# Five expert loads cut into sixteen-row and eight-row transfers, and a rearranged start of the value projection, in a one-core encoder layer

## The reference

```python
xn = rms_norm(h, norm1_w)
proj = xn @ w_in
q, k, v, r, a_low, hy_in, gates = jnp.split(proj, IN_SPLITS, axis=-1)
o_gla = gla_branch(q, k, v, r, a_low, gla_gate_w2, gla_gate_b, gla_norm_w)
kern = hyena_filters(L, hy_freq, hy_ffn_w1, ...)      # sin(fr * (z @ w1 + b1)), then w2, then w3
merged = sigmoid(g_gla) * (o_gla @ w_branch_gla) + sigmoid(g_hy) * (o_hy @ w_branch_hy)
h = h + merged @ w_out
for e in range(N_EXPERTS):                            # 32 experts
    gu = ht @ w_gate_up[e] + b_gate_up[e]             # 1024 x 2048 weights
    act = gate * sigmoid(SWIGLU_ALPHA * gate) * (up + 1.0)
    out = out + combine[:, e:e + 1] * (act @ w_down[e] + b_down[e])
```

## Time and profile before

| | |
|---|---|
| median of three runs | 1238.31 us |
| profiled execution, its own time | 1237.29 us |
| its span, first to last instruction | 1235.4 us |
| granted TensorE clock, mean | 0.999 |
| TensorE matmul busy | 1160.8 us (94%) |
| DVE, ACT busy | 420.2 us (34%), 266.9 us (22%) |
| bytes moved by DMA | 455.25 MB, mean 368 GB/s |

### The profile page before, as it was taken

The page is one execution under the profiler, slowest core; times in us unless marked ns, Lnnn a source line. Parts: engine busy times, 40 slices in busy tenths (PEclk is TensorE's granted clock), DMA queues, the critical chain, the costliest instruction groups (busy, mean ns, idle before and its releaser), DMA issues.

```text
span 1235.4 us, 13704 instructions
## 1 busy us (share of the span) xinstructions
PE 1160.8 (94%) x5828; PEld 599.6 (49%) x5828; DVE 420.2 (34%) x703; ACT 266.9 (22%) x422; POOL 0.2 (0%) x4
## 2 busy tenths in 40 slices
PE   7999999999999999999999889888988898889987
PEld 6899968888533443443343324333433333333332
DVE  6777878756421221222112112111221121111112
ACT  6866546344210000010010001000100010000002
POOL 0000000000000000000000000000000000000000
PEclk9999999999999999999999999999999999999999
DMA  9454425698999999999999999999999999999996
GB/s 322 147 157 151 148 91 171 217 399 340 365 425 428 427 428 428 427 429 425 429 426 429 428 428 428 427 428 428 427 428 425 429 427 429 427 429 427 427 426 263
DMA packets 67292, 455.25 MB, mean 368 GB/s; under 512 B 6970, under 2 KB 23771, under 8 KB 39966
## 3 DMA queue, kind: packets, MB, share of 16 engines
q1 hardware_dynamic: 65654, 454.06, 89.8%
q10 hardware_dynamic: 1576, 0.29, 0.1%
HBM read 453.29 MB, written 1.05 MB: 368 GB/s over the span
## 4 chain that ended last, share of the span: by engine, by line
PE 64%; DMA 32%; DVE 2%; issue 1%; ACT 1%; DVEq 0%; ACTq 0%
DMA ring<-in_w_gate_up 28%; PE bank L1201 18%; PE bank L1219 12%; PE total L902 6%; PE bank L902 5%; PE total L890 4%; PE bank L890 4%; DMA ring<-in_w_down 3%; PE bank L960 2%; PE bank L1187 2%; PE bank L979 1%; PE total L1233 1%; PE total L1201 1%; PE bank L1208 1%; PE total L950 1%
## 5 line engine op out<-in xcount | busy, mean ns | idle before, releaser
L1201 PE MATMUL bank<-ring,hy_area 128*64 128x512 f32 x1984 | 444.6, 595 | 43.2 <-DMA ring<-in_w_gate_up 43.2
L1201 PEld LDWEIGHTS bank<-ring,hy_area 128*64 128x64 f32 x1984 | 136.8, 137 | 331.4 <-issue 244.6
L1219 PE MATMUL bank<-ring,xn_area 128*64 128x512 f32 x992 | 220.1, 595 | 0.3 <-DMA ring<-in_w_down 0.3
L2119 DVE TENSOR_SCALAR qk_area<-bank 128x512 f32<-128x512 f32 x31 | 21.4, 692 | 361.3 <-PE bank L1201 361.3
L1219 PEld LDWEIGHTS bank<-ring,xn_area 128*64 128x64 f32 x992 | 68.4, 137 | 134.6 <-issue 122.8
L1682 ACT ACTIVATE qk_area<-qk_area 128x512 f32<-128x512 f32 x32 | 20.2, 630 | 456.7 <-DVE qk_area L2119 456.7
L2130 DVE SCALAR_TENSOR_TENSOR xn_area_r<-bank,tmp_area,xn_area_r 128x512 fp32r<-128x512 f32 x31 | 23.3, 751 | 200.5 <-ACT xn_area_r L1693 200.5
L1823 DVE TENSOR_TENSOR front_r<-ring,slot_r 128x1024 fp32r<-128x1024 f32 x60 | 73.1, 1222 | 22.2 <-ACT slot_r L1493 22.2
L1493 ACT CAST slot_r<-ring 128x1024 fp32r<-128x1024 f32 x60 | 62.8, 1049 | 43.5 <-PE bank L902 23.2
L1693 ACT ACTIVATE xn_area_r<-bank,tmp_area 128x512 fp32r<-128x512 f32 x31 | 21.3, 687 | 234.9 <-PE bank L1219 221.0
L979 PE MATMUL bank<-tmp_area_r 128*128 128x512 f32 x124 | 38.0, 426 | 12.8 <-issue 8.6
(11 more groups left out here) (397 smaller groups left out, 1253.2 us busy)
## 6 DMA issues: line engine op xcount, KB each, us to landing
ring<-in_w_gate_up SPq DMA_DIRECT2D x116, 2048.0 KB, 37.0
ring<-in_w_down SPq DMA_DIRECT2D x54, 2048.0 KB, 38.9
ring<-in_w_in SPq DMA_DIRECT2D x31, 1024.0 KB, 5.7
ring<-in_w_gate_up SPq DMA_DIRECT2D x22, 1024.0 KB, 9.4
ring<-in_w_down SPq DMA_DIRECT2D x19, 1024.0 KB, 9.9
ring<-in_w_branch_gla SPq DMA_DIRECT2D x4, 1024.0 KB, 5.2
ring<-in_w_branch_hy SPq DMA_DIRECT2D x4, 1024.0 KB, 7.7
ring<-in_w_out SPq DMA_DIRECT2D x4, 1024.0 KB, 6.3
```

Of the source, the lines that this page charges most:

```text
L1201: last = pe.matmul(to[bk][half * CAP:(half + 1) * CAP, :], xeT[:, j, q, :], where(j, c), start=False, stop=(j == GU_CH - 1), skip_group_ch ...
L1219: last = pe.matmul(banks[to][half * CAP:(half + 1) * CAP, :], half_of(turned, f), where(j, c * D + half * 512), start=(f == 0), stop=(f == ...
L2119: nc.vector.tensor_scalar(gate, made[0][:, :], LIMIT, None, ALU.min).then_inc(gate_ready, 1)
```

## The change

Three edits.

**Split loads.** Of the 170 loads of 2 MB, five (`[8::34]` of the list that starts at the 37th chunk: chunks 52, 120, 188, 256 and 324) are issued as nine DMAs, cut by rows, that is by SBUF partitions: seven transfers of 16 rows, r, r + 8, ... r + 120 for r from 0 to 6, and the rows 7, 15, ... in two transfers of 8, below 64 and from 64 on. The same slots are written, and the arrival counts grow by 16 for each DMA.

**The filter between the transposes.** The filter's first matmul moves to between the eight transposes of the first half of x and the first of the second half. It takes a bank at that place, so later tiles take others. The second layer's weights have a semaphore of their own.

**Units as their parts arrive.** `first_unit` becomes `early_unit(u)` for the first three units: high by high first, then high by low, then low by high, each by blocks, and ACT tells of each half of a group of `xhat`'s high part. The second chunk is loaded in two halves by units, and the rest of the table and `w_a` come behind it.

```diff
+STRIDE = 8
+SPLIT = tuple(n for n, width in LOADS if width == 2)[8::34]
+def row_parts(n):
+    if n not in SPLIT:
+        return [slice(0, P)]
+    return [slice(r, P, STRIDE) for r in range(STRIDE - 1)] + [slice(h + STRIDE - 1, h + P // 2, STRIDE) for h in (0, P // 2)]
@@ expert_arrivals
-        count[s] += 16
+        count[s] += 16 * len(row_parts(n))
@@ tiles_of
+    if stage == ("xT", 0):
+        return ["filter1", "xT0"]
+    if stage == ("filter", 1):
+        return []
@@ front, on SP
-                if c == 0:
+                if c < 2:
                     for i in range(UNITS_PER_CHUNK):
-                        sp.dma_start(unit_of(i), src[:, 2 * i:2 * i + 2, :]).then_inc([first_loaded, front_loaded[0]][i], 16)
+                        sp.dma_start(unit_of(2 * c + i), src[:, 2 * i:2 * i + 2, :]).then_inc([first_loaded[c], front_loaded[c]][i], 16)
@@ moe, on SP
-                sp.dma_start(ring[:, s * SLOT:(s + width) * SLOT], rows_of(*CHUNK_ORDER[n], width)).then_inc(moe_loaded[s], 16)
+                src = rows_of(*CHUNK_ORDER[n], width)
+                for rows in row_parts(n):
+                    sp.dma_start(ring[rows, s * SLOT:(s + width) * SLOT], src[rows, :]).then_inc(moe_loaded[s], 16)
@@ loads of the start, on SP
-                if c == 0:
+                if c == 1:
                     sp.dma_start(tab[:, P:], ins["shape_table"][:, P:]).then_inc(rest_loaded, 16)
-                if c == 1:
                     sp.dma_start(w_a.rearrange("p (b n) -> p b n", b=DB),
@@ on TensorE
-            def first_unit():
+            def early_unit(u):
...
+                for m, (act, w) in enumerate(((a_hi, hi), (a_hi, lo), (a_lo, hi))):
+                    if m == 1:
+                        pe.wait_ge(w_parts_ready, u + 1)
+                    elif m == 2:
+                        emptied(pe, f"xT{u}")
+                    for i in range(2):
+                        if m == 0:
+                            pe.wait_ge(xn_hi_ready, 2 * u + i + 1)
+                        for a in range(TB):
+                            last = pe.matmul(bank(f"v0{a}")[:, :], act[:, 2 * u + i, a * P:(a + 1) * P], w[:, i, :],
+                                             start=(u == 0 and m == 0 and i == 0), stop=False)
+            def first_filter():
+                pe.wait_ge(filt_loaded, 16 * 2)
+                pe.matmul(begin("filter1")[0:FFN, 0:SEQ], w1, zfeat, start=True, stop=True).then_inc(fill("filter1"), 1)
@@ transposes
+                        if a == 0 and at[0] == 0:
+                            first_filter()
@@ xT, on ACT
-                        last = nc.scalar.mul(parts_of["xn"][0][:, 2 * n + k, :], bank(f"xT{n}")[:, k * SEQ:(k + 1) * SEQ], col(C_N1 + 2 * n + k))
-                    last.then_inc(xn_hi_ready, 1)
+                        nc.scalar.mul(parts_of["xn"][0][:, 2 * n + k, :], bank(f"xT{n}")[:, k * SEQ:(k + 1) * SEQ],
+                                      col(C_N1 + 2 * n + k)).then_inc(xn_hi_ready, 1)
```

More of the change, by code:

```diff
@@ L536, in build @@
         rest_loaded = sem("rest_loaded")
-        first_loaded = sem("first_loaded")
+        first_loaded = [sem(f"first_loaded{c}") for c in range(2)]
         filt_loaded = sem("filt_loaded")
+        second_filt_loaded = sem("second_filt_loaded")
         wa_loaded = sem("wa_loaded")
@@ L904, in unit_passes @@
                 return last
-            def first_unit():
+            def early_unit(u):
                 a_hi, a_lo = parts_of["xn"]
[L909 to L913, removed]
+                hi, lo = unit_hi(u), unit_of(u, as_r["front"])
+                pe.wait_ge(w_hi_ready, u + 1)
+                if u == 0:
+                    for a in range(TB):
+                        begin(f"v0{a}")
                 for m, (act, w) in enumerate(((a_hi, hi), (a_hi, lo), (a_lo, hi))):
                     if m == 1:
-                        pe.wait_ge(w_parts_ready, 1)
+                        pe.wait_ge(w_parts_ready, u + 1)
                     elif m == 2:
[L918 to L922, removed]
+                        emptied(pe, f"xT{u}")
+                    for i in range(2):
+                        if m == 0:
+                            pe.wait_ge(xn_hi_ready, 2 * u + i + 1)
+                        for a in range(TB):
+                            last = pe.matmul(bank(f"v0{a}")[:, :], act[:, 2 * u + i, a * P:(a + 1) * P], w[:, i, :],
+                                             start=(u == 0 and m == 0 and i == 0), stop=False)
                 last.then_inc(unit_used, 1)
+            def first_filter():
+                pe.wait_ge(filt_loaded, 16 * 2)
+                pe.matmul(begin("filter1")[0:FFN, 0:SEQ], w1, zfeat, start=True, stop=True).then_inc(fill("filter1"), 1)
             def token_major(kind, half, u):
@@ L1013, in _ @@
                                                     xhat[:, a, (2 * n + k) * P:(2 * n + k + 1) * P], ident)
+                        if a == 0 and at[0] == 0:
+                            first_filter()
                     last.then_inc(fill(f"xT{at[0]}"), 1)
-                elif kind == "filter":
-                    n = f"filter{at[0]}"
-                    t = begin(n)
-                    if at[0] == 1:
-                        pe.wait_ge(filt_loaded, 16 * 4)
-                        i = pe.matmul(t[0:FFN, 0:SEQ], w1, zfeat, start=True, stop=True)
-                    else:
-                        pe.wait_ge(sin_ready, 1)
-                        i = pe.matmul(t[:, 0:SEQ], w2, s1, start=True, stop=True)
-                    i.then_inc(fill(n), 1)
+                elif stage == ("filter", 2):
+                    pe.wait_ge(sin_ready, 1)
+                    pe.wait_ge(second_filt_loaded, 16 * 2)
+                    pe.matmul(begin("filter2")[:, 0:SEQ], w2, s1, start=True, stop=True).then_inc(fill("filter2"), 1)
                 elif kind == "proj":
                     project(*at)
-                elif stage == UNITS[0]:
-                    first_unit()
+                elif stage in UNITS[:3]:
+                    early_unit(at[2])
                 elif kind == "tok":
@@ L1456, in _ @@
             for k in range(2):
-                sc.dma_start(w2[:, k * FFN:(k + 1) * FFN], ins["hy_ffn_w2"]).then_inc(filt_loaded, 16)
+                sc.dma_start(w2[:, k * FFN:(k + 1) * FFN], ins["hy_ffn_w2"]).then_inc(second_filt_loaded, 16)
             def sumsq(src, scratch, dst):
@@ L1488, in _ @@
                     j, = at
-                    s, v = front_arrival(j // UNITS_PER_CHUNK) if j else (first_loaded, 16)
+                    s, v = (first_loaded[j // 2], 16) if j in (0, 2) else front_arrival(j // UNITS_PER_CHUNK)
                     sc.wait_ge(s, v)
@@ L1833, in _ @@
                     n, = at
-                    what, ready, first_col = ("xn", xn_hi_ready, C_N1 + 2 * n) if kind == "xT" else ("ogla", ogla_hi_ready, C_GN)
-                    dve.wait_ge(ready, n + 1)
+                    what, first_col = ("xn", C_N1 + 2 * n) if kind == "xT" else ("ogla", C_GN)
+                    if kind == "xT":
+                        dve.wait_ge(xn_hi_ready, 2 * (n + 1))
+                    else:
+                        dve.wait_ge(ogla_hi_ready, n + 1)
                     hi, lo = parts_of[what]
```

## The result

| | before | changed | ratio, 95% interval |
|---|---|---|---|
| median, four runs each | 1238.04 us | 1286.84 us | 1.0395 [1.0382, 1.0408] |
| profiled execution, its span | 1237.29, 1235.4 us | 1287.67, 1285.8 us | |
| granted clock, mean | 0.999 | 0.984 | |

What follows compares the result with a forecast made beforehand. From 340 us the DMA stream was taken to bound the kernel, bytes over rate. 1237.29 + 25.1 (rate) - 1.5 (redistribution) - 0.3 (front) = 1260.6, or 1261.6 from the median; predicted 1261 us, range 1234 to 1275.

Steps and rivals of the forecast that it cites:

- What bounds the kernel: Whole kernel: from 340 us the DMA stream at 427 GB/s sets the end; before that, TensorE's front does.
- (a) Issue: Split loads: SP's nine issues take 3.0 us, hidden by the 37 us that loads lie queued; cost 0.
- (b) The rate: Split loads: transfers touching few partitions run at 211 GB/s, losing 5.03 us each, 25.1 us for five.
- the bound of 42.7: Upper case of the split loads' rate term: at 156 GB/s, 8.53 us lost each, 42.7 us.
- (c) Redistribution: Split loads' 8-row transfers: work moves between two sets of eight engines, -3.07 to +3.07 us; -1.5 taken.
- The rival with 0.06: Split loads: extra rows fall on the eight engines already late, each load ends 0.61 us later; 1241.1 us, chance 0.06.
- The front: Kernel start: filter's matmul costs some 0.45 us, TensorE loses idle time; -0.3 us taken, bounds -1.3 and +0.6.
- The wait of 0.35 us ahead of the filter: Front: TensorE idles 0.35 us before the filter's first layer in the kernel before, and the change removes it.
- ACT's part: Front: ACT's 1.49 us wait for unit 2's weights goes; copies before the gates come about half a microsecond earlier.
- That the stride spreads the rows: Rival for the split loads: no rate loss, and late engines relieved by up to 3.07 us; 1234.9 us, chance 0.22.
- The signs named: Half rate shows as GB/s well under 427 at share 1.0, five times; TensorE's waits grow up to 25 us, before 600 us.

Runs made afterwards that it cites:

- three single splits: Kernel before with one split load only, the first, third or last of the five: 1245.6, 1246.45 and 1249.0 us.
- Five in a row: Kernel before with five consecutive split loads, the 77th to the 81st of the 2 MB loads: 1268.75 us, ratio 1.0252.
- the uneven cut: Kernel before with the five loads each as three transfers of 32 rows, every fourth, and the rest as 8, 8 and 16: 1247.1 us, ratio 1.0077.
- the front alone: Changed kernel with all 170 loads of 2 MB whole, only the front's edits left: 1238.6 against 1237.55 us, ratio 1.0006.

## Why the forecast was half right

- **What bounds the kernel: right.** From 340 us the end is bytes over rate. The loss of three single splits, scaled to five, is within 1 us of the measured one.
- **(a) Issue, 0: right within 2.5 us.** Five times eight DMAs with 128 rows each cost 2.5 us in all.
- **(b) The rate: right; the size of the term: wrong. This is the step that failed.** The prediction has: "At 211 GB/s a split load takes 2.097 / 0.211 = 9.94 us, in place of 4.91: 5.03 us lost, five times, 25.1 us." The rate in the phase is 176 to 217 GB/s, as the earlier trace rows have it. But the step charges the slow rate to the split load's bytes alone. The engines are 2 to 7 us apart, so those ahead and behind carry whole loads during the phase, and these are slowed too. Measured: 8.2, 8.9 and 11.6 us for a load, 48.8 for five, outside even the bound of 42.7. Five in a row, where the neighbours are few, cost 6.2 each, near the step's 5.0. The rows that the step went by already had a slowed neighbour in them. This is what moved in the slow 4 us of the earlier trace rows, 18.5 to 22.5 us of the kernel before:

```profile
DMA packets 237, 0.84 MB, mean 211 GB/s; under 512 B 59, under 2 KB 59, under 8 KB 198
```

  The two 64-row transfers hold 0.52 MB of the 0.84, in packets of 4 KB. 237 - 198 = 39 packets are of 8 KB, and these are rows of the 128-row decay table (L790, 1024 KB), which is issued behind them: in the trace each of these takes 0.51 to 0.77 us there, against 0.31 from 23 us on. So a whole transfer crawled too, and the slow stretch lost 4 x (1 - 211 / 427) = 2.0 us. By the step's own reckoning, half rate for the bytes of the few-row transfers (4 x 32 KB and 2 x 256 KB, 0.66 MB) loses 1.5 at most. The same bytes say that it was the form of 64 adjoining rows that the earlier trace rows show at half rate: the 16-row transfers, named as "the form that went slowly", are at most 0.13 MB of them.
- **(c) Redistribution, -1.5: wrong sign.** The two 8-row transfers make the five loads 5.1 to 7.5 us slower than eight of 16 rows, and the uneven cut is 9.6 us slower than four free transfers of 32. The rival with 0.06, "the extra rows fall on the eight engines that are late already", is the one that the landings bear out (13.3 us apart, not 6.9). The loss is more than its 3.07, as transfers of few rows are slow besides. That the fetches of instructions make the engines uneven, as the prediction supposed, fits as well (last section).
- **The front, -0.3: not told from 0** (+1.1 us, within the interval of no change), but the steps were off. The filter took 1.11 us where I had 0.45, and unit 0 took 4.73 us (11.28 to 16.01) where I had 2.85, as durations at the full clock were carried to a place where the change kept the clock low. The wait of 0.35 us ahead of the filter is not TensorE's: the earlier trace rows show no wait there, and the trace has it for the loading of weights, which runs beside the matmuls. ACT's part came as named: the wait gone, the copies 0.30 us earlier (0.5 named). What the sum lacked is that 2 us of delay at 24 us are worth 1 us or less at the end.
- **Rivals.** That the stride spreads the rows is out; had it been every fourth row, it would have been right. The signs named (rate under 427 with the share at 1.0, five times, waits from before 600 us) were all seen; the waits grew by 34.2 us and not up to 25.

## To carry to other kernels

In a stream that DMA bounds, a transfer is cut so that it keeps the form of its neighbours (all 128 rows by columns, or every second or fourth row); anything else is tried by itself before it is put in the loop. When a resource is shared, price the time for which it is held and everything that moves in it, not the bytes of the one that holds it. And a duration read at full clock holds only where the engine's work ahead of it is left as it was.

## What was not expected

- One slow transfer slows all DMA traffic of the core: at 176 to 221 GB/s the share stays near 1.0, whole loads included, for 14 us or more, where the load itself needs 4.9 at full rate.
- The spread between the first and last of sixteen parts grows through the kernel before, 2.1 us at 400 us to 6.8 at 1070, with no split load in it. It does so mainly in three steps, 2.4 to 3.6, 4.0 to 5.2 and 5.6 to 6.9 us. At each step an instruction fetch falls (531.0, 753.4 and 992.3 us), which is every eighth of the 47, and the three took 1.0 us each. So it seems that every eighth fetch falls on the same late engine. No run tested it.
- TensorE's granted clock falls when it waits for such a load: 0.56 and 0.50 in the stretches 744 to 752 above, where it was busy 0 and 3.02 of 4 us, and full again from 756. With five splits the mean is 0.984. What this costs at the end was not separated: the four stretches account for 46 of the 50.4 us of the changed kernel's span, and the later start of the stream for 1.3 more (the span of the front alone is 1236.7 us).
- One matmul of 33 rows between transposes put off the full clock by 4 to 5 us (15.3 in the changed kernel against 10.2 before; 15.5 with the front alone against 11.4 without the move) and put `a_low`'s matmul 1.8 us later (24.32 against 22.55).
